# Projecting the latent tiles in the background of the sparse branch, and norms, queries, keys and values in one region

## The reference, cut to what matters

```python
h = rms_norm(x, g_norm)
# sparse branch (a): 8 heads of 64, every query attends to the 128 keys chosen by an index
q, k, v, qi, ki, wi, z_a = slices of h @ w_in
y_a = dsa_attention(rope(norm(q)), rope(norm(k)), v, qi, ki, wi)
merged  = sigmoid(h @ w_gate[0]) * ((y_a * silu(z_a)) @ w_branch[0])
# latent branch (b): 8 heads of 64 + 32 (rope), keys and values from a compressed latent
cq  = rms_norm(h @ w_cq, g_cq)            # 384 = 3 tiles of 128 features
ckv = rms_norm(h @ w_ckv, g_ckv)          # 256 = 2 tiles
q   = cq @ w_uq                           # 8 heads of 96
k_nope, v = ckv @ w_ukv                   # 8 heads of 64 + 64
y_b = causal_attention(rope(norm(q)), rope(norm([k_nope, k_rope])), v)
merged += sigmoid(h @ w_gate[1]) * ((y_b * silu(z_b)) @ w_branch[1])
# third branch, then  out = x + merged @ w_out
```

## Time and profile before

| | us |
|---|---|
| median of 3 runs | 1931.8 |
| lowest, highest | 1928.23, 1931.84 |
| profiled execution, its own time | 1929.16 |
| span of its instructions | 1927.4 |
| PE busy in the span | 1733.2 (90%) |
| DVE, ACT, POOL busy | 885.3, 701.9, 727.8 |
| mean granted TensorE clock | 0.945 |

### The profile page before, as it was taken

The page is one execution under the profiler, slowest core; times in us unless marked ns, Lnnn a source line. Parts: engine busy times, 40 slices in busy tenths (PEclk is TensorE's granted clock), DMA queues, the critical chain, the costliest instruction groups (busy, mean ns, idle before and its releaser), DMA issues. The chain is left out here.

```text
span 1927.4 us, 25419 instructions
## 1 busy us (share of the span) xinstructions
PE 1733.2 (90%) x10328; PEld 1304.2 (68%) x10328; DVE 885.3 (46%) x1462; ACT 701.9 (36%) x1182; POOL 727.8 (38%) x376
## 2 busy tenths in 40 slices
PE   6999968889998999999999987889787789987999
PEld 4866648768785878888788864644574456775777
DVE  5658774447523455333113807956212864313231
ACT  4334442233424432322233322224434255344431
POOL 5423323315540445555444535300323611452242
PEclk9999989989999999999999998969888889998999
DMA  4312110004330223322233420100212010432131
GB/s 168 129 55 60 61 35 24 3 15 147 115 98 22 88 77 102 96 91 94 88 99 98 135 78 22 50 16 6 71 53 73 11 44 12 131 115 72 60 104 55
DMA packets 39572, 138.56 MB, mean 72 GB/s; under 512 B 4384, under 2 KB 5664, under 8 KB 38304
## 3 DMA queue, kind: packets, MB, share of 16 engines
q1 hardware_dynamic: 39456, 136.93, 22.4%
HBM read 132.72 MB, written 4.19 MB: 71 GB/s over the span
## 5 line engine op out<-in xcount | busy, mean ns | idle before, releaser
L352 POOL TENSOR_TENSOR parts<-ring,parts 128x1024 fp32r<-128x1024 f32 (+3 forms) x251 | 571.6, 2281 | 946.6 <-ACT parts L343 946.2
L390 PE MATMUL banks<-h_hi,parts 128*128 128x512 f32 x1096 | 476.7, 435 | 31.2 <-ACT a_gate L570 9.8
L391 PE MATMUL banks<-h_lo,parts 128*128 128x512 f32 x1096 | 439.4, 401 | 0.0
L392 PE MATMUL banks<-h_hi,parts 128*128 128x512 f32 x1096 | 438.9, 400 | 0.0
L343 ACT CAST parts<-ring 128x1024 fp32r<-128x1024 f32 (+3 forms) x251 | 244.8, 979 | 234.2 <-PE banks L392 213.6
L390 PEld LDWEIGHTS banks<-h_hi,parts 128*128 128x128 f32 x1096 | 210.5, 192 | 113.3 <-issue 60.1
L391 PEld LDWEIGHTS banks<-h_lo,parts 128*128 128x128 f32 x1096 | 210.8, 192 | 57.8 <-issue 12.8
L392 PEld LDWEIGHTS banks<-h_hi,parts 128*128 128x128 f32 x1096 | 210.6, 192 | 49.9
L2617 ACT CAST ffn_act_hi<-ffn_gate 128x512 fp32r<-128x512 f32 x22 | 13.7, 621 | 167.1 <-DVE ffn_gate L2516 167.1
L2573 DVE TENSOR_TENSOR ffn_raw<-banks,ffn_root 128x512 f32<-128x512 f32 x22 | 15.2, 692 | 125.3 <-PE banks L392 125.2
L390 PE MATMUL banks<-ffn_act_hi,parts 128*128 128x512 f32 x176 | 69.8, 396 | 3.2 <-DVE ffn_gate L2516 3.2
(11 more groups left out here) (539 smaller groups left out, 3120.5 us busy)
## 6 DMA issues: line engine op xcount, KB each, us to landing
ring<-weights SPq DMA_DIRECT2D x211, 512.0 KB, 3.5
ring<-weights SPq DMA_DIRECT2D x24, 256.0 KB, 2.6
ring<-weights SPq DMA_DIRECT2D x8, 384.0 KB, 3.1
x<-xT SPq DMA_DIRECT2D x2, 1024.0 KB, 6.0
x<-xT SPq DMA_DIRECT2D x1, 2048.0 KB, 7.8
x_spill<-x SPq DMA_DIRECT2D x2, 1024.0 KB, 4.8
x<-x_spill SPq DMA_DIRECT2D x1, 2048.0 KB, 7.6
outT<-x SPq DMA_DIRECT2D x8, 256.0 KB, 2.0
```

Source lines behind the costliest of these rows:

```text
L352: self.nc.gpsimd.tensor_tensor(self.parts[:, t % PARTS, 1, 0:w], self.ring[:, t % SLOTS, 0:w], self.parts[:, t % PARTS, 0, 0:w].bitcast(F3 ...
L390: nc.tensor.matmul(out, w.hi, x.hi, start=first, stop=False)
L391: nc.tensor.matmul(out, w.hi, x.lo, start=False, stop=False)
L392: return nc.tensor.matmul(out, w.lo, x.hi, start=False, stop=last)
```

## The change

The five `b_c` tiles move in the weight plan from behind the branch tiles of branch a to behind its gate tiles, and become the last five jobs of the background of branch a (17 jobs, 136 steps instead of 96). `CHOOSE_STEPS` goes from 64 to 70. The stages `close_branch(0)`, `b_c` projection, norms with `b_uq`, `b_uk` and `b_uv` become one stage, `close_sparse`. In it PE issues 8 branch tiles, two sums of squares after the third (a matmul with a matrix of ones in float32, so that no transposes of the roots are needed), 8 `b_uq`, `b_uk` by pairs of heads, and `b_uv`; six banks rotate. The norm is made with two square roots on ACT and two reciprocals on DVE over 128x512. `b_k`, `b_v` and the halves of the latent are reserved earlier, the raw latent lies in the room of `b_k`, and the split branch output lies over `x`.

```diff
-CHOOSE_STEPS = 64
+CHOOSE_STEPS = 70
...
-    merge_tiles(0)
+    gate_tiles(0)
     feats("b_c", w2, C_CQ, QR + KVR)
+    branch_tiles(0)
...
-def gates(k, name, z, sg):
+def gates(k, name, z, sg, latent=()):
-    return Background(k, [(name, z[:, t, :]) for t in range(BW // P)] + [("gate", sg[:, m, :]) for m in range(DT)])
+    return Background(k, [(name, z[:, t, :]) for t in range(BW // P)] + [("gate", sg[:, m, :]) for m in range(DT)] +
+                      [("b_c", c) for c in latent])
...
+def close_sparse(k, y, z, sg, merged, background, latent):
...
+    background.finish(gating)
...
+    with k.stage() as block:
...
+        @block.tensor
+        def _(pe):
+            for m in range(DT):
+                freed(pe, m)
+                feature_major(yh, 4)(k, pe, first + m, bank(m))
+                if m == 2:
+                    pe.wait_ge(*G("squares_added").ge(3))
+                    for total, b in zip(totals, SUMS):
+                        nc.tensor.matmul(k.banks[b], k.const("ones"), total, start=True, stop=True).then_inc(*G("summed").inc())
+            for h in range(BH):
+                freed(pe, DT + h)
+                feature_major(ch, 3)(k, pe, uq + h, bank(DT + h), None if h else ready)
...      # 4 pairs of b_uk, then 4 token tiles of b_uv, the same way
+        @block.scalar
+        def _(act):
+            square(0, totals[0])
+            square(1, squares[0])
+            square(2, squares[1])
+            square(3, totals[1])
+            gate(0)
+            act.wait_ge(*G("squares_added").ge(1))
+            square(4, squares[0])
+            for m in range(1, DT):
+                gate(m)
+                if m in (2, 5):
+                    k.split_high(act, first + 1 + m // 3 + LEAD)
+            k.split_high(act, first + 3 + LEAD)
+            root(0)
+            root(1)
+            k.split_high(act, first + 5 + LEAD)
+            for i in range(3):
+                high(i)
+            k.split_high(act, first + 7 + LEAD)
+            for i in (3, 4):
+                high(i)
+            k.split_high(act, uq + LEAD)
+            for h in range(BH):
+                k.split_high(act, uq + h + 1 + LEAD)
+                act.wait_ge(k.tile_used, uq + h + 1)
+                nc.scalar.copy(q[0:BQK, h, :], bank(DT + h)[0:BQK, :]).then_inc(*G("bank_taken_act").inc())
+            for pair in range(BH // 2):
...      # two copies of keys per pair
+            k.split_high(act, uv + LEAD)
+            for t in range(ST):
...      # one copy of values per token tile
+            k.split_high(act, k.used + LEAD)
+        @block.vector
+        def _(dve):
+            add(2, totals[0], squares[0])
...
+            add(3, totals[0], squares[1])
+            weigh(0)
+            add(5, totals[1], squares[0])
+            weigh(1)
+            weigh(2)
+            recip(0)
+            weigh(3)
+            for i in range(3):
+                normed(i)
+            low(0)
+            weigh(4)
+            low(2)
+            weigh(5)
+            recip(1)
+            normed(3)
+            normed(4)
+            weigh(6)
+            low(4)
+            weigh(7)
...      # eight copies of the rope key
+        @block.gpsimd
+        def _(pool):
+            k.split_low(pool, first + 5 + LEAD)
+            low(1)
+            k.split_low(pool, first + 7 + LEAD)
+            low(3)
+            k.split_low(pool, k.used + LEAD)
...
-                background = gates(k, "a_z", z, sg)
+                background = gates(k, "a_z", z, sg, [latent.c[:, t, :] for t in range(5)])
...
-        close_branch(k, 0, y, z, sg, merged, background)
+        merged = k.sbuf(start.ctx, "merged", [P, DT, S])
+        latent.more(k)
+        close_sparse(k, y, z, sg, merged, background, latent)
...
-                jobs = [Job("b_c", feature_major(k.h), "act", lambda e, cc, b, t=t: nc.scalar.copy(c[:, t, :], b)) for t in range(5)]
-                project(k, jobs)
-                with ExitStack() as n_ctx:
-                    normed = Norms(k, n_ctx, room=sg, groups=...)
-                    project(k, [Job("b_uq", feature_major(ch, 3), "act", ...) for h in range(BH)], normed)
...      # the stage for b_uk
-                project_tokens(k, "b_uv", ch[:, 3:5, :], S, lambda act, t, b: nc.scalar.copy(v[:, t, :], b), ktiles=2)
```

More of the change, by code:

```diff
@@ L121, in weight_plan, with gate_tiles, branch_tiles, merge_tiles @@
     w2 = "w_in_2"
-    def merge_tiles(n):
+    def gate_tiles(n):
         for m in range(DT):
             plan.append(("gate", feature_tile(w2, C_GATE + n * D + m * P)))
+    def branch_tiles(n):
         for m in range(DT):
             plan.append(("branch", feature_tile("w_branch_2", m * P, P, BW, n * BW)))
+    def merge_tiles(n):
+        gate_tiles(n)
+        branch_tiles(n)
     feats("a_qi", w2, C_QI, 512)
@@ L268, in __init__ @@
         self.holes = [(-(-nc.sbuf_base // 32) * 32, nc.sbuf_top // 32 * 32)]
-        self.small = 0
+        self.small, self.placed = 0, {}
     def counter(self, name):
@@ L293, in sbuf, with over @@
         ctx.callback(self.release, start, start + size)
+        self.placed[name] = start
         return self.nc.alloc_sbuf_tensor_at(name, shape, dt, offset=start)
+    def over(self, name, shape, dt, other, offset=0):
+        return self.nc.alloc_sbuf_tensor_at(name, shape, dt, offset=self.placed[other] + offset)
     def release(self, start, end):
@@ L2757, in __init__ @@
         self.h = halves(k, self.h_ctx, k.fresh("h"), [P, DT, S])
-        self.merged = k.sbuf(self.ctx, "merged", [P, DT, S])
         self.y, self.z = k.sbuf(self.branch, "a_y", [P, 4, S]), k.sbuf(self.branch, "a_z", [P, 4, S])
@@ L3029, in take @@
             dve.wait_ge(*k.counter("gate_ready").ge(m + 1))
-            if n == 0:
-                return nc.vector.tensor_tensor(merged[:, m, :], bank, sg[:, m, :], ALU.mult)
             chain(nc.vector.tensor_tensor(sg[:, m, :], bank, sg[:, m, :], ALU.mult))
@@ L3041, in close_branch, with __init__, more, ready @@
                 first_act=gating.act_gates)
-def sparse_branch(k, merged, start):
+class Latent:
+    def __init__(self, k):
+        self.at, self.c_ctx = ExitStack(), ExitStack()
+        self.key = k.sbuf(self.at, "b_k", [P, BH, S], high=True)
+        self.c = self.key[:, 0:5, :]
+    def more(self, k):
+        self.v = k.sbuf(self.at, "b_v", [P, ST, BH * BV])
+        self.ch = halves(k, self.c_ctx, "b_c", [P, 5, S])
+class LatentReady:
+    def __init__(self, k):
+        self.k = k
+    def ready(self, i):
+        G = self.k.counter
+        return G("norm_low").ge((i + 1) // 2) if i % 2 else G("low_dve").ge(i // 2 + 1)
@@ L3045, in sparse_branch @@
+def sparse_branch(k, start, latent):
     nc = k.nc
@@ L3086, in sparse_branch, with latent_branch @@
             attend(k, units, AHD ** -0.5, background, 1)
-        close_branch(k, 0, y, z, sg, merged, background)
-def latent_branch(k, merged):
+        merged = k.sbuf(start.ctx, "merged", [P, DT, S])
+        latent.more(k)
+        close_sparse(k, y, z, sg, merged, background, latent)
+    return merged
+def latent_branch(k, merged, latent):
     nc = k.nc
     with ExitStack() as ctx:
[L3093 to L3098, removed]
-            q_scale = k.sbuf(at_ctx, "b_q_scale", [P, ST, BH])
-            with ExitStack() as c_ctx:
-                ch = halves(k, c_ctx, "b_c", [P, 5, S])
-                c = q
-                jobs = [Job("b_c", feature_major(k.h), "act", lambda e, cc, b, t=t: nc.scalar.copy(c[:, t, :], b)) for t in range(5)]
-                project(k, jobs)
-                with ExitStack() as n_ctx:
[L3108 to L3147, removed]
-                project_tokens(k, "b_uv", ch[:, 3:5, :], S, lambda act, t, b: nc.scalar.copy(v[:, t, :], b), ktiles=2)
@@ L3149, in latent_branch @@
+        with latent.at as at_ctx:
+            latent.c_ctx.close()
+            y, z, sg = k.sbuf(ctx, "b_y", [P, 4, S]), k.sbuf(ctx, "b_z", [P, 4, S]), k.sbuf(ctx, "b_gate", [P, DT, S])
+            q, key, v = k.x, latent.key, latent.v
+            q_scale = k.sbuf(at_ctx, "b_q_scale", [P, ST, BH])
             with ExitStack() as rope_ctx:
@@ L3206, in second_block @@
     with start.ctx as ctx:
-        merged = start.merged
         with start.h_ctx:
             k.h = start.h
-            sparse_branch(k, merged, start)
-            latent_branch(k, merged)
+            latent = Latent(k)
+            merged = sparse_branch(k, start, latent)
+            latent_branch(k, merged, latent)
             memory_branch(k, merged)
```

100 lines of the change are left out of this document (added).

## The result

The changed kernel takes 1898.88 us (median of 4 runs, 1897.22 to 1901.0), the kernel before 1931.82 (4 runs, 1928.23 to 1934.61): a ratio of 0.9837, 95% interval 0.9826 to 0.9849. It is 33 us faster; forecast were 48, to 1884, with a range that ended at 1898. The profiled execution took 1898.49 us, its span is 1896.7: 30.7 us less than the span of the profiled execution before.

The account below looks back on a forecast made before the run. PE, busy 90% of the span, was taken to bound the kernel. Terms 0.9 - 0.8 + 8.2 - 56.2 = -47.9 us took 1929.16 to 1881.3; with 2.6 for the median, 1884 us. Forecast 1879 to 1891, wider range 1876 to 1898.

Parts of the forecast that it names:

- The joined stage: First branch matmul to head norms of branch b: 51.8 us of PE, then 5.1; 56.9 instead of 113.1, -56.2 us.
- a drain: ACT's table loads in the joined stage: the skill's 1.38 us per switch, judged absent; with it the sum would be -45.
- `finish`: Last attention matmul of branch a to first branch matmul: 21 remaining steps, 16.2 us instead of 8.07, +8.2 us.
- the attention's clock: Branch a attention, four job boundaries: 2.2 us wait plus 1.1 for clock drops each, 13.2 us; stage 93.6 against 94.4.
- The start: Start of branch a's attention: clock stays up because the gap shrinks to about 0.3 us; first head copy after 16.4 us.
- the six steps: Choice of keys: six more background steps cross one job boundary with a 0.77 us wait; cost 0.9 us.
- The first one: Rival: clock still falls at the start of branch a's attention, 30.1 us instead of 16.4, total 1897; chance 0.14.
- The rule of the Trainium skill: PE at the start of branch a's attention: full clock returns after a short busy stretch; by it the sum would be -34.

Follow-up runs that it names:

- the copy ahead of the exp: Changed kernel, but in the attention ACT copies a finished background tile out before the next unit's exp: 1865.61 us. The same edit in the kernel before: 1914.38 us.
- the background part alone: Changed kernel with the stages behind `finish` as before; latent tiles still projected in the background, 70 steps in the choice of keys: 1918.76 us.
- the 128-row runs: Branch a scores taken over all 128 rows of two heads instead of 64 of one: changed kernel 1871.99 us, kernel before 1914.65 us.

## Why the prediction was wrong, step by step

**Where it held.** The joined stage was forecast as a race and ran as one: 51.9 us from PE's first to its last matmul (forecast 51.8), one wait, at the third `b_uq` tile, of 0.66 us (forecast 0.5), released by POOL's low half; 5.44 us before the head norms (forecast 5.1). No drain shows beside the table loads, as in the earlier trace rows: here too the load begins right behind the squares (1392.82 and 1392.84), and ACT's next work right behind the load (1394.12 and 1394.13). By the figure of the Trainium skill (ScalarE: Activation LUTs, What ACT_TABLE_LOAD costs) for a drain, an estimate is that this chain would have come 2.8 us later; this trace doesn't agree. `finish` came out at 16.4 for 16.2.

**The step that failed: the attention's clock.** It is the term "4 x 3.3 = 13.2 us (bounds 4 x 1.85 = 7.4 and 4 x 4.7 = 18.8)": a wait of 2.2 us, "and 1.1 more on average because such a wait can drop the clock for a while". The waits came as forecast, the falls were mis-sized. In the second trace of the changed kernel a wait makes its head 7.0 us longer where the clock falls and 2.3 where it doesn't; the first one lies ahead of the first head copy (23.6 us, against 17.5 - 0.9 = 16.6 with the copy ahead of the exp). Together 3 x 7.0 + 2.3 = 23.3 us, 5.8 for each, above the bound; the background part alone has the same. In the first trace, with the fall at the start, it is 13.2 us up to the first copy and 8.1, 7.0 and 2.3 in the heads: 30.6 us. The rest of the sum held: 16.6 for 16.4 to the first copy, 9.9 us for a head, 4.7 for the tail. So the attention took 104.0 and 111.3 us instead of 93.6.

The prediction shows no row for its 1.1 us. The row that bears on it gives a fall of 3.4 us at the second wait of before:

```profile
1306.40:1309.81 3.41, 3.41 (x7) 1.43 (x8) 0.00 (x0) 0.50 (x2) 1.27 (x1) 0.50 0.16 50
```

That wait stood at unit 11, where the product with the values of a head follows at once, as it did at the short falls of the changed kernel with 64 steps. Behind units 5, 13, 21 and 29 PE has two more units of scores on 64 rows, transposes and background steps before such a product, and there the falls, where one came, lasted 6.8 to 13.7 us. The long fall at the start of before had already shown that the clock can stay down in that work. I used that row for the start alone. That the place in the head sets the length fits these falls; no run tested it by itself.

**The start.** "If the clock stays up because the gap before is gone" was right in five of six traces with 70 steps and scores on 64 rows (first head copy 17.5 to 23.7 us after the start) and wrong in the changed kernel's first one (29.8). The gap was 0.8 us in the kernel before with 70 steps and 1.9 in the five others, forecast 0.3. The step that missed the gap: the six steps cross a change of job, which I priced with PE's wait of 0.77 us, but ACT then also casts the next weight tile, POOL makes its low half until 1262.17, and SP issues the next load behind it, all ahead of the barrier. That moved the end by 2.7 us instead of 0.9. With the old order of weights it is 1.6 us, because the tile due there is a branch tile of half the width; the latent tile that now stands in its place is the change's own price.

**The rivals.** The first one (clock falls at the start, 1897) gave the nearest number, but its reason was only part of the truth: a second execution without that fall took 1900.85. That this number came so near is luck. Its chance of 0.14 is no clear error: the fall at the start was there in one of the six traces. No rival had several long falls inside the attention. The rule of the Trainium skill (TensorE: Matmul & The Clock Gate, the HAM clock gate) that the full clock comes back after a short busy stretch fits the attention of branch a in the 128-row runs (3.4 to 6.8 us at 1.2 GHz). With scores on 64 rows it fits some falls (3.4 to 6.8 us at the last unit of a head, 6.8 once at unit 5) and not others (10 to 34 us, PE busy). The forecast was right that the rows don't bear the rule out at the start of branch a; the mistake was to take only short falls for the waits inside.

**Where the gain comes from.** In the order kernel before, 70 steps, background, joined stage, the medians are 1929.6, 1913.3, 1918.8 and 1898.9 (the last on another chip): -16.3, +5.4, -19.9 us. The projection of the latent tiles in the background, the part named first in the change, cost time while the waits at its changes of job brought the clock down. With the copy ahead of the exp the changed kernel is 33 us faster still. The background part without the joined stage wasn't run with that copy, so what it is worth alone then isn't shown.

**What stays open.** Scores over 128 rows change two things at once: the rows in use, and how soon the next matmul starts (heads without a wait are 1.4 us shorter). Which of the two keeps the clock up was not separated. Nor was it settled why a gap of 1.9 us brought the clock down at the start in one of five traces, why a wait of 2.2 us did so at three of four places, or why it fell twice among pauses of at most 0.71 us. Between the trace with the fall at the start and the others the work lay 3 to 9 us otherwise in time. Each kernel but the changed one has one trace, and whether the two longer executions with 70 steps alone lost their 7 us by such a fall isn't known. Where these shifts come from, before the second block, was not followed.

## What to carry to other kernels

An idle gap of PE has two prices: its length, and the time at the lower clock behind it. Read the second from a stretch with the same kind of matmuls behind the gap, and take a range, since the same gap brought falls of different lengths or none. Where an engine that works in order both feeds PE and frees its bank, put the freeing copy first: here that one order was worth as much as the whole change. And a step that crosses into a new job brings that job's loads and splits ahead of the next barrier.

## What the runs showed of the hardware

PE at 1.2 GHz can stay there for 30.7 to 34.1 us while it is 86 to 95% busy with float32 scores on 64 rows, transposes and few full matmuls; the same list of instructions with scores on 128 rows was back at 2.4 GHz after 6.8 us. The same kernel with scores on 64 rows also had falls of 3.4 and 6.8 us. At waits of 2.2 us at full clock the clock fell in most cases, not in all; at the waits of 0.5 to 0.9 us that the copy ahead of the exp leaves at the changes of job in branch a it never did. Short pauses are no guarantee: in two traces it fell for 3.4 us in a head without background, where the longest pause was 0.71 us. Scores on 64 rows weren't cheaper than on 128: a head with four background steps took 9.9 us with the first and 8.5 with the second, one without steps 7.7 with either.
